# DeltaNet branch: the two directions' small products of both doublings issued alternately

## The chip, the cores and the metric

The kernel runs on one core of a Trainium2 chip. The metric is the time of one execution on the device in microseconds (us). The engines are TensorE (PE in the rows, its weight loads PEld), VectorE (DVE), ScalarE (ACT), GpSimd (POOL) and the DMA queues. Each engine takes its own instructions in the order in which the program has them, and semaphores tie the engines together.

## The reference, cut to what matters

One encoder layer: four token mixers, a gated merge, a memory cross attention and a mixture of experts, in float32. The change lies in the fourth mixer, a gated DeltaNet that runs over the sequence forward and backward. For each chunk of 64 tokens and each of 4 heads it solves a unit lower triangular system and then carries a state on:

```
a_mat = jnp.where(strict, bc[..., None] * kk * decay, 0.0) + jnp.eye(c)
sol = lax.linalg.triangular_solve(a_mat, rhs, left_side=True, lower=True, unit_diagonal=True)
...
o_f = gdn_scan(q, k, v, beta[:, :, 0], log_a[:, :, 0])
o_b = _flip(gdn_scan(_flip(q), _flip(k), _flip(v), ...))
```

## The kernel before

The kernel handles DeltaNet in 8 steps i of 128 tokens (two chunks of 64), for both directions d (0 forward, 1 backward) and NH = 4 heads h. VectorE has inverted the 32x32 diagonal blocks of each triangular matrix. Two doublings make the whole inverse of them: the first ("level 5") joins 32x32 blocks to 64x64, the second ("level 6") joins 64x64 blocks to 128x128. A doubling is a product y (L1023), a negated copy of it, and a product with it, zy (L1040); level 5 also has a third product xy (L1033), which makes the transposed block.

TensorE's part of a step is `gdn_c` with parts 0 to 6, all under `for d in range(2)`:

- part 0: `gbc` (L1014, two full-size products), then y of level 5. Per direction: wait for the copies of the step before, `gbc`, wait for GpSimd's `z` (L2807), y.
- part 1: wait for VectorE's `yn` (L2406, two instructions per direction), then xy and zy of level 5.
- part 2: wait for VectorE's `z` (L2411 once and L2413 twice per direction, which copy xy and zy out of PSUM), then y of level 6.
- part 3: wait for ScalarE's `yn` (L1731), then zy of level 6.
- part 4: wait for ScalarE's `z` (L1735), then `wk` (L1047), which ScalarE copies out (L1739).
- part 5: v (L1053, L1061); VectorE makes `vn` from it (L2419). Part 6: u and o (L1067, L1072, L1075); VectorE updates the state (L2424, L2429), and o is copied out by ScalarE (L1743) for i below 4, by VectorE (L2432) from i = 4 on. The next step's `gbc` of the same direction waits for that copy.

The small products of level 5 are 32x32 on 32 rows and 32 columns of the array, those of level 6 64x64. The operands' partitions fix the place:

```
OFF = ((slice(64, P), slice(0, 64)), (slice(0, 64), slice(64, P)))
OFF32 = [[(slice(64 * b + 32, 64 * b + 64), slice(64 * b, 64 * b + 32))[::1 - 2 * d] for b in range(2)] for d in range(2)]
```

So a level-5 y or zy uses two 32x32 places of the array for one direction and two others for the other direction; xy uses one place for each direction; a level-6 product uses one 64x64 place for each direction. A float32 product is two passes (two MATMUL rows of the trace). The semaphore of TensorE's DeltaNet work is one counter that rises in program order.

The order of all engines' work is a hand-written list of steps. Between the parts it puts pieces of the merge projection (L787, six 128x512 products, "a filler"): one filler after each of parts 1 to 5, none between parts 0 and 1 and none between part 6 and the next part 0. In steps 0 to 2 VectorE also has pieces of the second half's block inversion (L2385, L2388) after parts 1, 2 and 4. After part 2 (from step 1 on) ScalarE issues the loads of the next step (L1774, L1782).

Of the kernel before, what the change touches and what calls it, by code (L numbers as in the profile page):

```python
# [29 lines left out]
NH = 4  # L30
# [273 lines left out]
def build(nc, A, out, known):  # L304
# [15 lines left out]
    with ExitStack() as ctx:  # L320
# [435 lines left out]
        def _(pe):  # L756
            for step in schedule:
# [240 lines left out]
                elif what == "gdn_c":  # L998
# [3 lines left out]
                    for d in range(2):  # L1002
# [13 lines left out]
                        if part in (0, 2):  # L1016
                            if part == 0:
                                pe.wait_ge(*po.at("z", i, d))
                            else:
                                pe.wait_ge(*v.at("z", i, d, 5))  # L1020
                            for h in range(NH):
                                for rows_y, cols_y in OFF32[d] if part == 0 else (OFF[d],):
                                    mm = nc.tensor.matmul(B0[rows_y, h, cols_y], NLT[s][d][cols_y, h, rows_y], NX[d][cols_y, h, cols_y],  # L1023
                                                          start=True, stop=True)
                            mm.then_inc(*q.mark("y", i, d, 5 + part // 2))
                        elif part in (1, 3):
                            lv = 5 + part // 2
                            pe.wait_ge(*(v if lv == 5 else a).at("yn", i, d, lv))
                            if lv == 5:
                                pe.wait_ge(*a.at("qd", i, d))  # L1030
                                rows_y, cols_y = OFF32[d][d]
                                for h in range(NH):
                                    mm = nc.tensor.matmul(B1[rows_y, h, cols_y], NZ_[d][rows_y, h, rows_y], NY[d][rows_y, h, cols_y],  # L1033
                                                          start=True, stop=True)
                                mm.then_inc(*q.mark("xy", i, d, lv))
                                if i:
                                    pe.wait_ge(*v.at("um", i - 1, d))
                            for h in range(NH):
                                for rows_y, cols_y in OFF32[d] if lv == 5 else (OFF[d],):
                                    mm = nc.tensor.matmul(B2[cols_y, h, rows_y], NY[d][rows_y, h, cols_y], NZ_[d][rows_y, h, rows_y],  # L1040
                                                          start=True, stop=True)
                            mm.then_inc(*q.mark("zy", i, d, lv))
# [1901 lines left out]
```

## Time and profile before

| what | value |
|---|---|
| time, 3 runs | 2054.76 us median (2052.96 to 2055.24) |
| the profiled execution's own time | 2065.67 us |
| its span, first to last instruction | 2063.9 us |
| TensorE busy | 1909.5 us, 93% of the span |
| VectorE / ScalarE / GpSimd busy | 1388.5 / 1083.7 / 324.1 us |
| L1023 on TensorE (y, both levels) | 384 passes in 15.0 us |
| L1040 on TensorE (zy, both levels) | 384 passes in 14.7 us |

The eight steps of parts 0 to 6 lie between 792 and 957 us of the span. A row of the timeline gives the start of a group of instructions, the time from the first start to the last end, and in brackets how long the engine had been idle before it and what released it. Since passes of TensorE overlap, a group's time less the last pass's own time is the time between its first and last start.

### The profile page before, as it was taken

The numbers are of one execution on the slowest core, as the hardware profiler recorded it, in microseconds if no ns is written. First come the engines' busy times: TensorE is split into PE (matmuls) and PEld (weight loads), VectorE is DVE, ScalarE is ACT, GpSimd is POOL, SyncE is SP. The second block draws the span as 40 slices with busy tenths as digits, with TensorE's granted clock in tenths as the row PEclk, the third lists the DMA queues.
The fourth block names the chain that finished last, engine by engine and source line by source line (L and its number), as shares of the span: only waits on it lengthen the run. The fifth ranks groups of instructions, "written<-read, shape, count | busy, mean of one in ns | idle before, by whom it ended". The sixth has DMA issues, their size and how long they took to land.

```text
span 2063.9 us, 33015 instructions
## 1 busy us (share of the span) xinstructions
PE 1909.5 (93%) x13076; PEld 1138.2 (55%) x13076; DVE 1388.5 (67%) x1831; ACT 1083.7 (53%) x1582; POOL 324.1 (16%) x285
## 2 busy tenths in 40 slices
PE   6999999999999999999999999895899999999991
PEld 3464565655544545767488855685355444444440
DVE  4555533799865687634643845437799999999986
ACT  4563223666656432223333534334588888888862
POOL 6000100344300523421000000000001111111102
PEclk9999999999999999999999999997899999999995
DMA  5411111212011352332321500403799999999976
GB/s 185 161 51 42 32 42 53 66 47 57 24 39 47 118 179 83 113 108 99 138 67 48 168 32 21 167 31 152 268 423 422 422 422 421 422 422 422 422 290 261
DMA packets 140522, 360.45 MB, mean 175 GB/s; under 512 B 38224, under 2 KB 91632, under 8 KB 113776
## 3 DMA queue, kind: packets, MB, share of 16 engines
q1 hardware_dynamic: 96608, 279.57, 35.7%
q10 hardware_dynamic: 34944, 46.14, 6.4%
q0 software_dynamic: 8848, 33.03, 4.1%
q8 instruction: 87, 1.43, 0.3%
q14 instruction: 35, 0.29, 0.0%
HBM read 307.85 MB, written 46.66 MB: 172 GB/s over the span
## 4 chain that ended last, share of the span: by engine, by line
PE 79%; DVE 9%; ACT 5%; issue 4%; DMA 1%; SPq 1%; DVEq 0%; ACTq 0%; POOL 0%; POOLq 0%
PE psum L787 40%; PE psum L1194 24%; ACT arena L1636 2%; PE psum L1183 1%; PE psum L1118 1%; PE psum L1093 1%; DVE arena L2288 1%; PE psum L917 1%; PE psum L1212 1%; PE psum L804 1%; PE psum L1053 1%; PE psum L989 1%; DMA arena<-in_w_in_dram 1%; PE psum L979 1%; PE psum L928 1%
## 5 line engine op out<-in xcount | busy, mean ns | idle before, releaser
L787 PE MATMUL psum<-arena 128*128 128x512 f16 (+2 forms) x6000 | 1016.6, 327 | 7.7 <-issue 2.8
L787 PEld LDWEIGHTS psum<-arena 128*128 128x128 f16 x6000 | 569.6, 98 | 391.5 <-issue 23.5
L1194 PE MATMUL psum<-arena 128*128 128x512 f16 x2304 | 513.5, 382 | 15.6 <-issue 12.5
L744 DVE SCALAR_TENSOR_TENSOR arena<-arena 128x2048 f16<-128x2048 f32 x192 | 437.6, 2286 | 57.9 <-ACT arena L738 57.6
L738 ACT ACTIVATE arena<-arena 128x2048 f16<-128x2048 f32 x192 | 365.5, 1908 | 69.6 <-DMA arena<-in_w_dram 42.9
L1194 PEld LDWEIGHTS psum<-arena 128*128 128x128 f16 x2304 | 224.7, 98 | 282.4 <-issue 24.7
L1944 DVE SCALAR_TENSOR_TENSOR arena<-arena 128x512 f16<-128x512 f32 (+1 forms) x185 | 124.9, 695 | 123.0 <-ACT arena L1358 122.6
L2847 POOL DMA_INDIRECT arena<-xhat,arena x32 | 67.5, 2109 | 842.1 <-PE psum L1183 446.0
L1358 ACT ACTIVATE arena<-arena 128x512 f16<-128x512 f32 (+1 forms) x212 | 127.0, 616 | 35.8 <-PE psum L787 11.4
L1379 ACT ACTIVATE arena<-psum,arena 128x512 f32<-128x512 f32 x64 | 43.8, 684 | 149.2 <-PE psum L787 149.1
L1443 ACT ACTIVATE arena<-psum 128x512 f32<-128x512 f32 (+3 forms) x51 | 29.9, 586 | 119.8 <-PE psum L787 119.8
L1407 ACT ACTIVATE arena<-arena 128x256 f32<-128x256 f32 x64 | 26.6, 416 | 108.9 <-DVE arena L1980 107.9
L2735 POOL TENSOR_SCALAR arena<-arena 128x512 f32<-128x512 f32 x27 | 57.5, 2129 | 138.8 <-ACT arena L1358 138.8
L2273 DVE CUSTOM_DVE_ANT_0 arena<-psum,arena 128x1024 f32<-128x1024 f32 x64 | 75.6, 1219 | 2.1 <-PE psum L904 2.0
L1968 DVE SCALAR_TENSOR_TENSOR arena<-arena,psum 128x512 f32<-128x512 f32 x64 | 43.8, 684 | 49.0 <-PE psum L787 34.8
L1636 ACT ACTIVATE arena<-arena 128x1024 f32<-128x1024 f32 x64 | 72.9, 1147 | 7.1 <-DVE arena L2273 7.0
L1998 DVE SCALAR_TENSOR_TENSOR arena<-psum,arena 128x512 f16<-128x512 f32 x36 | 24.8, 690 | 61.5 <-ACT arena L1443 31.0
L1980 DVE SCALAR_TENSOR_TENSOR arena<-psum,arena 128x512 f32<-128x512 f32 x32 | 22.1, 690 | 64.3 <-PE psum L787 64.3
L1645 ACT ACTIVATE arena<-psum 128x512 f16<-128x512 f32 x64 | 34.7, 595 | 55.1 <-PE psum L917 34.3
L2807 POOL TENSOR_TENSOR arena<-arena 128x512 f32<-128x512 f32 x32 | 34.8, 1106 | 128.0 <-DMA arena<-gdn_inv 82.6
L1859 ACT ACTIVATE arena<-psum 128x512 f32<-128x512 f32 x64 | 38.1, 597 | 14.2 <-PE psum L1194 13.9
L1183 PE MATMUL psum<-arena 128*128 128x128 f32 x256 | 34.4, 278 | 10.3 <-DMA arena<-xhat,arena 10.3
(390 smaller groups left out, 2089.6 us busy)
## 6 DMA issues: line engine op xcount, KB each, us to landing
arena<-in_w_dram SPq DMA_DIRECT2D x192, 1024.0 KB, 11.9
arena<-in_merge_w_dram SPq DMA_DIRECT2D x64, 256.0 KB, 3.0
yrows<-arena ACTq DMA_DIRECT2D x32, 512.0 KB, 7.9
arena<-in_w_in_dram SPq DMA_DIRECT2D x48, 256.0 KB, 2.8
gdn_lq<-arena ACTq DMA_DIRECT2D x8, 1024.0 KB, 4.0
arena<-gdn_lq ACTq DMA_DIRECT2D x8, 1024.0 KB, 5.1
arena<-in_xattn_wkv_dram SPq DMA_DIRECT2D x32, 256.0 KB, 2.8
yrows<-arena POOLq DMA_DIRECT2D x1, 7680.0 KB, 24.3
```

The lines of the kernel that those rows point to most:

```text
L738: nc.scalar.activation(half_of(pieces(e, m)[0], half), half_of(XLAND[m], half), ACT.Copy, scale=WS).then_inc(w_hi[m], 1)
L744: nc.vector.scalar_tensor_tensor(half_of(lo, half), half_of(XLAND[m], half), WS, half_of(hi, half), ALU.mult, ALU.subtract).then_inc(w_lo[ ...
L787: mm = nc.tensor.matmul(bank[prt[0]:prt[1], c0:c1], lhs[a](k), rhs[b](k), start=(k == 0 and a + b == 0), stop=(k == nk - 1 and a == 1))
L1183: tr = nc.tensor.transpose(PS[:, k // 4, (k % 4) * P:(k % 4) * P + P], xs[:, k, :], ident)
L1194: mm = nc.tensor.matmul(PS[:, bank, :], left[a][:, k, :], right[b][:, k, columns], start=k + a + b == 0, stop=(k == n - 1 and a == 1))
L1358: S.activation(W[i % 2][0][:, 2 * j:2 * j + 2, 0:wide], LAND[c % NLAND][:, :, 0:wide], ACT.Copy, scale=WS).then_inc(*act_hi.mark(c))
L1379: S.activation(SG[gate_no[n] % 2], bank, ACT.Tanh, scale=0.5 / WS, bias=half_b[:, 8 * kind[1] + kind[2]:8 * kind[1] + kind[2] + 1]).then_i ...
L1636: S.activation(DS[u % 2][:, m, :], DS[u % 2][:, m, :], ACT.Exp, scale=-1.0, bias=d_mx[u % 2][:, m:m + 1], accum_out=d_l[u % 2][:, m:m + 1])\
L1944: V.scalar_tensor_tensor(W[i % 2][1][:, 2 * j:2 * j + 2, 0:wide], LAND[c % NLAND][:, :, 0:wide], WS, W[i % 2][0][:, 2 * j:2 * j + 2, 0:wid ...
L2273: V.tensor_tensor_reduce(out=DS[u % 2][:, m, :], in0=PS[:, 2 + 2 * m:4 + 2 * m, :].rearrange("p a b -> p (a b)"), in1=DWH[:, 896 - P * qt: ...
L2735: G.tensor_scalar(landed_c, landed_c, WS, None, ALU.mult).then_inc(*counter("pool_w_scaled").mark(chunk))
L2847: G.indirect_dma_start(XR[e % 2], None, XH_D, bass.IndirectOffsetOnAxis(IDX[:, e:e + 1], 0)).then_inc(rows_in[e % 2], 16)
```

## The change

The per-direction loop keeps the waits and the full-size products. The small products of both levels are taken out of it and issued after it, head by head and direction by direction within a head. So all waits of both directions now stand ahead of the first small product of a part. No instruction is added or taken away, and the lists of VectorE, ScalarE, GpSimd and the DMA queues are as they were.

```diff
                         if part in (0, 2):
-                            if part == 0:
-                                pe.wait_ge(*po.at("z", i, d))
-                            else:
-                                pe.wait_ge(*v.at("z", i, d, 5))
-                            for h in range(NH):
-                                for rows_y, cols_y in OFF32[d] if part == 0 else (OFF[d],):
-                                    mm = nc.tensor.matmul(B0[rows_y, h, cols_y], NLT[s][d][cols_y, h, rows_y], NX[d][cols_y, h, cols_y],
-                                                          start=True, stop=True)
-                            mm.then_inc(*q.mark("y", i, d, 5 + part // 2))
+                            pe.wait_ge(*(v.at("z", i, d, 5) if part else po.at("z", i, d)))
                         elif part in (1, 3):
-                            lv = 5 + part // 2
-                            pe.wait_ge(*(v if lv == 5 else a).at("yn", i, d, lv))
-                            if lv == 5:
+                            pe.wait_ge(*(a.at("yn", i, d, 6) if part == 3 else v.at("yn", i, d, 5)))
+                            if part == 1:
                                 pe.wait_ge(*a.at("qd", i, d))
...
+                    if part in (0, 2):
+                        for h in range(NH):
+                            for d in range(2):
+                                for rows_y, cols_y in of[d]:
+                                    mm = nc.tensor.matmul(bank[d][0][rows_y, h, cols_y], NLT[s][d][cols_y, h, rows_y], NX[d][cols_y, h, cols_y],
+                                                          start=True, stop=True)
+                                if h == NH - 1:
+                                    mm.then_inc(*q.mark("y", i, d, 5 + part // 2))
+                    if part == 1:
+                        for h in range(NH):
+                            for d in range(2):
+                                rows_y, cols_y = OFF32[d][d]
+                                mm = nc.tensor.matmul(bank[d][1][rows_y, h, cols_y], NZ_[d][rows_y, h, rows_y], NY[d][rows_y, h, cols_y],
+                                                      start=True, stop=True)
+                                if h == NH - 1:
+                                    mm.then_inc(*q.mark("xy", i, d, 5))
+                    if part in (1, 3):
+                        for h in range(NH):
+                            for d in range(2):
+                                for rows_y, cols_y in of[d]:
+                                    mm = nc.tensor.matmul(bank[d][2][cols_y, h, rows_y], NY[d][rows_y, h, cols_y], NZ_[d][rows_y, h, rows_y],
+                                                          start=True, stop=True)
+                                if h == NH - 1:
+                                    mm.then_inc(*q.mark("zy", i, d, 5 + part // 2))
```

On TensorE, parts 0 and 1 of one step stand like this before (a row is a run of like instructions; the names in brackets are the semaphores waited for: `pool_gdn`, `vec_gdn`, `act_gdn` are the DeltaNet counters of GpSimd, VectorE and ScalarE):

```order
L1014 MATMUL psum<-arena 128x128 [waits pool_gdn,act_gdn,vec_gdn]
L1014 MATMUL psum<-arena 128x128
L1023 MATMUL psum<-arena 32x32 [waits pool_gdn]
L1023 MATMUL psum<-arena 32x32 x7
L1014 MATMUL psum<-arena 128x128 [waits pool_gdn,act_gdn,vec_gdn]
L1014 MATMUL psum<-arena 128x128
L1023 MATMUL psum<-arena 32x32 [waits pool_gdn]
L1023 MATMUL psum<-arena 32x32 x7
L1033 MATMUL psum<-arena 32x32 [waits act_gdn,vec_gdn]
L1033 MATMUL psum<-arena 32x32 x3
L1040 MATMUL psum<-arena 32x32 [waits vec_gdn]
L1040 MATMUL psum<-arena 32x32 x7
```

And in the changed kernel, whose L1066, L1074 and L1082 are y, xy and zy:

```order
L1014 MATMUL psum<-arena 128x128 [waits pool_gdn,act_gdn,vec_gdn]
L1014 MATMUL psum<-arena 128x128
L1014 MATMUL psum<-arena 128x128 [waits act_gdn,pool_gdn,vec_gdn]
L1014 MATMUL psum<-arena 128x128
L1066 MATMUL psum<-arena 32x32 [waits pool_gdn]
L1066 MATMUL psum<-arena 32x32 x15
L1074 MATMUL psum<-arena 32x32 [waits vec_gdn,act_gdn]
L1074 MATMUL psum<-arena 32x32 x7
L1082 MATMUL psum<-arena 32x32 x16
```

The forward direction's y now stands behind the backward direction's `gbc` and its waits, and its xy and zy behind the backward direction's `yn`.

Parts 2 and 3 on TensorE, before:

```order
L1023 MATMUL psum<-arena 64x64 [waits vec_gdn]
L1023 MATMUL psum<-arena 64x64 x3
L1023 MATMUL psum<-arena 64x64 [waits vec_gdn]
L1023 MATMUL psum<-arena 64x64 x3
L787 MATMUL psum<-arena 128x512 x6
L1040 MATMUL psum<-arena 64x64 [waits act_gdn]
L1040 MATMUL psum<-arena 64x64 x3
L1040 MATMUL psum<-arena 64x64 [waits act_gdn]
L1040 MATMUL psum<-arena 64x64 x3
```

And now, at the same place of a step:

```order
L1066 MATMUL psum<-arena 64x64 [waits vec_gdn]
L1066 MATMUL psum<-arena 64x64 x7
L787 MATMUL psum<-arena 128x512 [waits vec_w_lo]
L787 MATMUL psum<-arena 128x512 x5
L1082 MATMUL psum<-arena 64x64 [waits act_gdn]
L1082 MATMUL psum<-arena 64x64 x7
```

What was one direction's four products and then the other's is now eight in alternation behind the waits of both (the filler's own wait, for the merge's weights, is one that it has in either kernel).

## Rows read from the trace of the kernel before

**Rows 1.** The page: the span, and the chain that ended last, by engine.

```profile
span 2063.9 us, 33015 instructions
...
PE 79%; DVE 9%; ACT 5%; issue 4%; DMA 1%; SPq 1%; DVEq 0%; ACTq 0%; POOL 0%; POOLq 0%
```

**Rows 2.** TensorE's waits, 790 to 950 us: us in total, times, longest us.

```profile
PE psum L1033 <- DVE arena L2406: 4.4, 8, 1.5
PE psum L1047 <- ACT arena L1735: 2.3, 2, 1.4
PE psum L1014 <- DVE arena L2432: 1.9, 4, 0.6
PE psum L1014 <- POOL arena L2820: 1.1, 1, 1.1
```

**Rows 3.** Timeline of TensorE, step 1, parts 0 and 1.

```profile
813.11 0.44 PE L1023 MATMUL psum<-arena 32*32 32x32 f32 x16
...
816.06 0.34 PE L1033 MATMUL psum<-arena 32*32 32x32 f32 x5 [1.50 <-DVE arena L2406]
...
816.69 0.34 PE L1033 MATMUL psum<-arena 32*32 32x32 f32 x5
...
817.22 1.47 PE L787 MATMUL psum<-arena 128*128 128x512 f16 x6
```

**Rows 4.** TensorE, step 1, part 2, cut at 818.895, at 819.08, and whole.

```profile
818.62 0.44 PE L1023 MATMUL psum<-arena 64*64 64x64 f32 x4
...
818.62 0.67 PE L1023 MATMUL psum<-arena 64*64 64x64 f32 x11
...
818.62 0.96 PE L1023 MATMUL psum<-arena 64*64 64x64 f32 x16
```

**Rows 5.** Timeline of VectorE, step 1: `yn`, then the copies of part 1.

```profile
815.39 1.24 DVE L2406 TENSOR_SCALAR arena<-psum 32x128 f32<-32x128 f32 x4
816.70 0.28 DVE L2411 COPY arena<-psum 32x128 f32<-32x128 f32 x1
...
817.85 0.61 DVE L2413 COPY arena<-psum 32x128 f32<-32x128 f32 x2
```

**Rows 6.** Timeline of TensorE, step 6, parts 0 and 1.

```profile
915.93 0.68 PE L1014 MATMUL psum<-arena 128*128 128x128 f32 x4 [0.34 <-DVE arena L2432]
916.54 0.34 PE L1023 MATMUL psum<-arena 32*32 32x32 f32 x10
...
917.69 0.34 PE L1033 MATMUL psum<-arena 32*32 32x32 f32 x5 [0.39 <-DVE arena L2406]
...
918.21 1.47 PE L787 MATMUL psum<-arena 128*128 128x512 f16 x6
```

**Rows 7.** Timeline of VectorE, step 6: o, then `yn` of both directions.

```profile
915.42 0.41 DVE L2432 TENSOR_TENSOR arena<-psum,arena 128x256 f32<-128x256 f32 x1
915.86 0.61 DVE L2406 TENSOR_SCALAR arena<-psum 32x128 f32<-32x128 f32 x2
917.03 0.60 DVE L2406 TENSOR_SCALAR arena<-psum 32x128 f32<-32x128 f32 x2 [0.56 <-PE psum L1023]
```

**Rows 8.** Timeline of ScalarE, step 6, parts 2 and 3.

```profile
922.01 0.69 ACT L1379 ACTIVATE arena<-psum,arena 128x512 f32<-128x512 f32 x1 [0.91 <-PE psum L787]
...
924.74 0.78 ACT L1735 ACTIVATE arena<-psum 64x256 f32<-64x256 f32 x2 [2.04 <-issue]
```

**Rows 9.** VectorE busy, 804 to 828.9 us: us, busy and count, clock, DMA.

```profile
804.00:828.90 24.90, 23.43 (x56) 1.00 0.23 65
```

**Rows 10.** Timeline, end of step 1: `vn` on VectorE and the weight load that waits.

```profile
828.92 0.76 DVE L2419 TENSOR_TENSOR arena<-psum,arena 128x256 f32<-128x256 f32 x2
829.40 0.53 PEld L1067 LDWEIGHTS psum<-arena 128*128 128x128 f32 x4 [0.22 <-DVE arena L2419]
```

**Rows 11.** Timeline of ScalarE, step 4, part 2: the loads of the next step.

```profile
879.64 2.79 ACTq L1782 DMA_DIRECT2D arena<-gdn_inv  x2
```

**Rows 12.** Timeline of TensorE, step 5: a filler and the part 2 behind it.

```profile
897.18 2.74 PE L787 MATMUL psum<-arena 128*128 128x512 f16 x6
899.85 1.26 PE L1023 MATMUL psum<-arena 64*64 64x64 f32 x16
```

**Rows 13.** TensorE in that stretch: us, busy and count, granted clock, DMA.

```profile
897.00:901.00 4.00, 4.00 (x41) 0.57 0.00 0
```

More of the change, by code:

```diff
@@ L1016, in _ @@
                         if part in (0, 2):
-                            if part == 0:
-                                pe.wait_ge(*po.at("z", i, d))
-                            else:
-                                pe.wait_ge(*v.at("z", i, d, 5))
-                            for h in range(NH):
-                                for rows_y, cols_y in OFF32[d] if part == 0 else (OFF[d],):
-                                    mm = nc.tensor.matmul(B0[rows_y, h, cols_y], NLT[s][d][cols_y, h, rows_y], NX[d][cols_y, h, cols_y],
-                                                          start=True, stop=True)
-                            mm.then_inc(*q.mark("y", i, d, 5 + part // 2))
+                            pe.wait_ge(*(v.at("z", i, d, 5) if part else po.at("z", i, d)))
                         elif part in (1, 3):
-                            lv = 5 + part // 2
-                            pe.wait_ge(*(v if lv == 5 else a).at("yn", i, d, lv))
-                            if lv == 5:
+                            pe.wait_ge(*(a.at("yn", i, d, 6) if part == 3 else v.at("yn", i, d, 5)))
+                            if part == 1:
                                 pe.wait_ge(*a.at("qd", i, d))
[L1031 to L1035, printed above, removed]
                                 if i:
                                     pe.wait_ge(*v.at("um", i - 1, d))
[L1038 to L1042, printed above, removed]
                         elif part == 4:
@@ L1078, in _ @@
                             mm.then_inc(*q.mark("o", i, d))
+                    bank = [[PS[:, 2 + 3 * d + b, :].rearrange("p (h n) -> p h n", h=NH) for b in range(3)] for d in range(2)]
+                    of = [OFF32[d] if part < 2 else (OFF[d],) for d in range(2)]
+                    if part in (0, 2):
[22 more added lines that the diff above has]
+                                    mm.then_inc(*q.mark("zy", i, d, 5 + part // 2))
                 elif what == "xattn_s":
```

## The prediction

> **What bounds the kernel now.** I read the page first: TensorE makes 79% of the chain that ended last [rows 1]. The change touches only the eight DeltaNet steps between 792 and 957 us, so the second view is who TensorE waits for there [rows 2]: for VectorE's `yn` (L2406) once in every step, 4.4 us, for ScalarE's `z` (L1735) twice, 2.3 us, and ahead of `gbc` (L1014) for the last copy of the step before, 1.9 and 1.1 us. Everything else in the stretch is TensorE's own work back to back. So a saving on TensorE counts if no other engine's result is late behind it, and a result that VectorE gives later counts as soon as no filler covers it. Then come the timelines of a step, TensorE beside VectorE, once for the early steps [rows 3, 5] and once for the late ones [rows 6, 7].
>
> **What alternation gives.** A group's time less its last pass is the time from first to last start. Level 6, 16 passes: the first 4 start within 0.44 - 0.22 = 0.22 us, the next 7 within 0.23 us (0.67 - 0.44), the last 5 within 0.29 us [rows 4]. The outer stretches have one direction running, about 58 ns a pass; in the middle both run and together start one in 33 ns at most (7 in 0.23). So the two 64x64 places work side by side without slowing each other, and today they overlap for only about three passes. In full alternation 8 passes of each need 8 x 58 = 0.46 us in place of 0.96 - 0.22 = 0.74 us: 0.28 us less. There are 16 such groups (parts 2 and 3 of 8 steps): 4.5 us off TensorE. Level 5 with one direction already uses two places: 16 passes in 0.44 - 0.19 = 0.25 us [rows 3], one start in 17 ns, against 0.15/4 = 37 ns where xy has one place alone (L1033 x5 in 0.34 us). No row has four places at work; I take it that they scale on, 32 passes in 0.25 us. Then part 1 for both directions takes what it takes for one now: from the start at 816.69 to the filler at 817.22, 0.53 us [rows 3].
>
> The Trainium skill, page "TensorE: Matmul & The Clock Gate", section "Wait — 56ns, not 53.3ns?", says that start to start never drops below about 25 ns however small the product. Its rule would leave level 5 nothing to gain; this trace disagrees at two places already, 17 ns, and it leaves level 6 alone, whose alternate starts are 29 ns apart.
>
> **What alternation costs, part by part.**
>
> Parts 0 and 1. In steps 1 to 3 VectorE is busy with the state until 815.39 while both y were done by 814.56, so the later forward y costs nothing, and `yn` of both directions still ends at 815.39 + 1.24 = 816.63 [rows 3, 5]. In the late steps it is otherwise. In step 6 VectorE makes the forward `yn` at 915.86, while TensorE is still at the backward `gbc`, which waited for L2432 [rows 6, 7]. Now the forward y stands behind that `gbc`: both y start at 916.54, end 0.25 + 0.19 us later, and VectorE starts the first `yn` where it now starts the second, at 917.03. One direction's `yn` (0.31 us x 2 = 0.62) moves from under the wait to behind it. Part 1 starts at 917.69 + 0.62. The same holds for steps 5 and 7, and for step 0 with GpSimd's L2820 in the place of L2432 [rows 2]. In step 4 the copy is ScalarE's and comes earlier: from the same chain I get 0.27. Sum on part 1's start: 4 x 0.62 + 0.27 = 2.75 us.
>
> Part 2. It waits for six copies on VectorE, three a direction. In step 1 they run from 816.70 to 817.85 + 0.61 = 818.46 [rows 5], because the forward products are done before the backward ones start. TensorE arrives at 818.62, hence 0.16 us of slack [rows 4]. Now no copy can begin before the joint part 1 is through: start 816.69, last start 0.40 later, 0.19 for the pass, 0.05 for the semaphore (816.63 to 816.69 above): 817.33. The six end at 817.33 + 1.76 = 819.09, part 2 starts at 819.14 in place of 818.62: 0.53 us in each step that is not stopped otherwise. What covers it now is the filler of 1.40 us, and that is too short by this much.
>
> **The steps added up** (change of TensorE's time, each step on top of the one before):
>
> - Step 0: 0.62 + 0.53 - 0.56 = +0.6.
> - Step 1: 0.53 - 0.56 = 0.0 at first. But VectorE is 1.2 us later and has almost no idle time to lose it, 23.43 us busy of 24.90 [rows 9]; `vn` ends at 829.68 and L1067's weights have already waited for it [rows 10]. So +0.5.
> - Step 2: ScalarE's `z` is already late by 1.4 us [rows 2]. ScalarE's chain hangs on the filler behind part 2 (L1379 in [rows 8] for step 6, alike here), which moves by 0.53 - 0.28; the saving of part 3 falls into that wait. +0.25.
> - Step 3: 0.53 - 0.56 = 0.0.
> - Step 4: 0.27 + 0.53 - 0.56 = +0.25 if ScalarE keeps up. Its load issues take 2.79 us behind L1731 [rows 11] and then release L1735; if they keep their length, the later part 2 comes through whole, +0.8. I take the middle, +0.5.
> - Step 5: the filler ran at half clock and took 2.74 us [rows 12], so it covers the copies: 0.62 - 0.56 = +0.05.
> - Step 6: 0.62 + 0.53 - 0.28 = +0.9, as in step 2, since L1379 and then L1735 stand on the filler [rows 8].
> - Step 7: 0.62 + 0.53 - 0.56 = +0.6.
>
> Sum +3.4 us. Behind the stretch TensorE leads the chain, so I let it through to the end whole. Bounds from the same rows: if VectorE's `vn` in step 1 and ScalarE in step 4 do not bite, +2.6; if step 5 has no slow filler, that step costs 0.53 more, and with step 4 at its upper end +4.2. Removing the two switches between small and full-size products in part 0 lies wholly under VectorE's work, hence nothing.
>
> **The clock.** In step 5 the granted clock fell to 0.5 of full (1.2 of 2.4 GHz; 0.57 is the mean of the stretch [rows 13]) right behind parts 0 and 1 of that step, in which TensorE has little but small products and waits, as in [rows 6]. It cost (2.74 - 1.47) + (1.26 - 0.96) = 1.6 us [rows 12]. The change makes just these thin stretches 0.6 us longer in four steps, so one more such drop is likely in some runs. I add 0.4 us for it, a quarter of a drop: +3.8 us. The profiled execution (2065.67 us) would become 2069.5; on the median, 2054.8 + 3.8 = 2058.6 us.
>
> **The rivals.**
>
> - Waits already there take it all. If joint y comes out before VectorE is free in the late steps too, and part 2's copies are not last, the 4.5 us of level 6 stay whole: 2050.3 us, faster. It decides at 0.16 us of slack ahead of part 2 [rows 4, 5]: the copies may begin no more than that later. Against it: VectorE's idle 0.56 us ahead of the backward `yn` [rows 7] shows that it does wait for y. 7%.
> - The gains and losses cancel, 2054 to 2056 us. If joint part 1 ends earlier than I take it (all its passes at 8 ns, 48 x 8 = 0.38 us at most), or the forward copies may start some 0.3 us sooner, part 2 loses 0.2 in place of 0.53. 13%.
> - Four places do not scale. If TensorE starts one level-5 pass in 17 ns at best, joint y takes 0.53 in place of 0.25 and joint part 1 0.80 in place of 0.40 us; that is 5 x 0.28 + 8 x 0.40 = 4.6 us more: 2063.2 us. No row excludes it. 8%. By the skill's 25 ns it would be 32 x 25 = 0.80 and 48 x 25 = 1.20 us, thus 5 x 0.55 + 8 x 0.80 = 9.2 us more, 2067.8 us; since a row has 17 ns I give it 1%.
> - One or two more clock drops in the median run: 1.6 us each, 2060.2 to 2061.8 us. 16%.
> - The forecast, 2057.2 to 2059.8 us: 55%.
>
> About 0.2% (4.1 us) is what a measurement of this kernel can tell from no change, and the forecast lies just inside it. Slower by more than that: the clock, the four places, and somewhat under half of the forecast's own range: 0.48. Within it: the rest of the forecast and the cancelling case, 0.45. Faster: 0.07. The range from 2054.5 to 2062.5 leaves out the first rival, the four places and some of the clock.
>
> **What would show it.** Level-6 groups at 0.68 us in place of 0.96 (right about the array); L1074 starting at least 0.6 us later behind `gbc` in steps 0, 5, 6 and 7 and not in 1 to 3; a new TensorE wait ahead of the 64x64 products for L2413's successor, 0.4 to 0.6 us in most steps, 3 to 4 us in sum; joint y of 32 passes at 0.44 us. It would be wrong if that wait is not there, or if the level-5 groups of 32 passes take 0.7 us and more.

## The result, and the profile after

The changed kernel takes 2069.72 us (median, 2067.86 to 2071.63) where the kernel before, on the same chip, takes 2053.86 us (2052.58 to 2055.24). The medians differ by 15.9 us, the kernel is **slower**; the ratio is 1.0073 (15.0 us), 95% interval 1.0057 to 1.0090. In a second measurement it was 1.0078 (1.0062 to 1.0093), and the medians differed by 15.8 us. The prediction said 2058.6 us, 2054.5 to 2062.5: the sign was right, the size a quarter of the real one, and the time is outside the range.

The page of the changed kernel, its span and the chain that ended last; these answer to [rows 1]:

```profile
span 2068.5 us, 33046 instructions
...
PE 78%; DVE 10%; ACT 5%; issue 4%; DMA 1%; SPq 1%; POOL 0%; DVEq 0%; ACTq 0%; POOLq 0%
```

The page hardly moved; the stretch of the DeltaNet steps did. Its ends are in the timeline of TensorE. Before, the first level-5 products and the last `o` products:

```profile
792.88 0.44 PE L1023 MATMUL psum<-arena 32*32 32x32 f32 x16
...
953.86 1.00 PE L1075 MATMUL psum<-arena 128*128 128x64 f32 x8
```

After, the same two:

```profile
792.12 0.45 PE L1066 MATMUL psum<-arena 32*32 32x32 f32 x32
...
966.11 1.00 PE L1056 MATMUL psum<-arena 128*128 128x64 f32 x8
```

From the first product to the start of the last one the stretch took 161.7 us before and 174.7 after, **13.0 us more**. The two profiled spans differ by less (4.6 us) because before's profiled execution lay 11 us above its median: behind the stretch, where both kernels do the same work, it took 1109.3 us, the changed kernel 1101.6. From here on "the stretch" is this piece, and every kernel is compared by it and by its ratio.

TensorE's waits in the stretch, 790 to 955 us, for [rows 2] (us in total, times, longest us):

```profile
PE psum L1074 <- DVE arena L2413: 14.0, 8, 2.6
PE psum L1014 <- DVE arena L2439: 3.8, 4, 1.2
PE psum L1028 <- ACT arena L1742: 3.0, 2, 1.8
PE psum L1066 <- DVE arena L2420: 1.6, 3, 0.5
PE psum L1014 <- POOL arena L2827: 1.3, 1, 1.3
PE psum L1048 <- DVE arena L2426: 0.8, 1, 0.8
```

L1074 is part 1 (before L1033), L2413 is `yn` (L2406), L1066 is y (L1023), L2439 the copy that `gbc` waits for (L2432). The wait of part 1 grew from 4.4 to 14.0 us, yet that is not a loss of 9.6: before, the forward products were done while TensorE waited for the backward `yn`, and now all eight steps wait with nothing in hand.

The granted clock, 792 to 952 us, first before, then after (us, busy time and count of PE, PEld, DVE, ACT and POOL, granted clock, DMA share, GB/s):

```profile
792.00:952.00 160.00, 150.09 (x1755) 110.62 (x1754) 89.82 (x238) 39.01 (x91) 56.59 (x77) 0.99 0.28 85
```

```profile
792.00:952.00 160.00, 135.89 (x1640) 96.01 (x1640) 86.70 (x233) 35.06 (x82) 53.57 (x73) 0.93 0.28 82
```

TensorE was busy 14 us less of the same 160 us, and its mean clock fell from 0.99 to 0.93. In the clock records of the trace the stretch of before has 3.4 us at the half level (1.2 of 2.4 GHz), that of after 23.9 us, in six places; four of them begin within 1.3 us of the start of part 1 of a step (steps 1, 3, 6 and 7), one begins 1.1 us ahead of it (step 5, 6.8 us long), and one lies in the middle of step 2. Over the whole execution the difference is small in these two profiles, 118.8 us at the half level before and 122.3 after; what a typical execution of before has is a matter of the control run below.

How one step looks now: TensorE in step 4, parts 0, 1, the filler and part 2, to be held against [rows 3, 4]:

```profile
879.82 0.37 PE L1066 MATMUL psum<-arena 32*32 32x32 f32 x24
881.84 0.34 PE L1074 MATMUL psum<-arena 32*32 32x32 f32 x11 [1.65 <-DVE arena L2413]
...
882.48 1.47 PE L787 MATMUL psum<-arena 128*128 128x512 f16 x6
884.49 0.68 PE L1066 MATMUL psum<-arena 64*64 64x64 f32 x16 [0.54 <-DVE arena L2420]
```

And VectorE beside it, `yn` of both directions and the six copies, for [rows 5]:

```profile
880.23 1.24 DVE L2413 TENSOR_SCALAR arena<-psum 32x128 f32<-32x128 f32 x4 [1.06 <-PE psum L1066]
882.58 0.28 DVE L2418 COPY arena<-psum 32x128 f32<-32x128 f32 x1 [1.11 <-PE psum L1082]
...
883.73 0.61 DVE L2420 COPY arena<-psum 32x128 f32<-32x128 f32 x2
```

Three things stand in these seven rows. The level-6 group takes 0.68 us in place of 0.96. TensorE begins part 1 at 881.84, but `yn` had ended at 880.23 + 1.24 = 881.47: 0.37 us, where before the same gap was 0.06 (816.63 to 816.69). The trace has this in other steps too: 0.05 to 0.06 us in all eight before, 0.36 to 0.39 in steps 1 to 7 and 0.26 in step 0 after. And part 2 waits 0.54 us for the copies although a filler stands ahead of it (1.40 us from its start to the next work).

TensorE in step 6, for [rows 6]:

```profile
922.63 0.68 PE L1014 MATMUL psum<-arena 128*128 128x128 f32 x4 [0.81 <-DVE arena L2439]
923.25 0.45 PE L1066 MATMUL psum<-arena 32*32 32x32 f32 x32
925.35 0.37 PE L1074 MATMUL psum<-arena 32*32 32x32 f32 x11 [1.65 <-DVE arena L2413]
...
926.12 2.74 PE L787 MATMUL psum<-arena 128*128 128x512 f16 x6
928.79 0.74 PE L1066 MATMUL psum<-arena 64*64 64x64 f32 x16
```

From the backward `gbc` to part 1 it is 2.72 us now, 1.76 before. The filler of six products takes 2.74 us, as in [rows 12] and not 1.47: the half clock. Because it lasts longer, part 2 behind it shows no wait.

### The profile page after: what moved, and what is told of

It reads as the page before. It is cut to its first block, busy times and chain, and to the rows that moved or that the text cites. A ratio compares the mean times of both kernels' runs of the same rounds, so it can differ in the third digit from the quotient of the medians.

```text
span 2068.5 us, 33046 instructions
## 1 busy us (share of the span) xinstructions
PE 1907.4 (92%) x13076; PEld 1133.0 (55%) x13076; DVE 1387.6 (67%) x1831; ACT 1084.1 (52%) x1582; POOL 322.8 (16%) x285
## 4 chain that ended last, share of the span: by engine, by line
PE 78%; DVE 10%; ACT 5%; issue 4%; DMA 1%; SPq 1%; POOL 0%; DVEq 0%; ACTq 0%; POOLq 0%
PE psum L787 40%; PE psum L1201 24%; ACT arena L1643 2%; PE psum L1190 1%; PE psum L1100 1%; PE psum L1125 1%; DVE arena L2295 1%; PE psum L917 1%; PE psum L804 1%; PE psum L1219 1%; PE psum L989 1%; PE psum L979 1%; DVE arena L2395 1%; DMA arena<-in_w_in_dram 1%; PE psum L928 1%
## 5 line engine op out<-in xcount | busy, mean ns | idle before, releaser
L787 PE MATMUL psum<-arena 128*128 128x512 f16 (+2 forms) x6000 | 1021.5, 328 | 7.1 <-DVE arena L2090 2.8
L787 PEld LDWEIGHTS psum<-arena 128*128 128x128 f16 x6000 | 570.0, 99 | 393.2 <-issue 28.2
L1866 ACT ACTIVATE arena<-psum 128x512 f32<-128x512 f32 x64 | 38.1, 597 | 14.2 <-PE psum L1201 14.1
## 6 DMA issues: line engine op xcount, KB each, us to landing
arena<-in_w_dram SPq DMA_DIRECT2D x192, 1024.0 KB, 11.9
```

What stands on the lines that cost most here:

```text
L787: mm = nc.tensor.matmul(bank[prt[0]:prt[1], c0:c1], lhs[a](k), rhs[b](k), start=(k == 0 and a + b == 0), stop=(k == nk - 1 and a == 1))
```

## The experiments

All ratios are to the kernel before on the same chip, with a 95% interval. That kernel's own median was 2061.1, 2059.8 and 2061.4 us on chips A, B and C and 2053.9 to 2054.7 us on chip D ("first" is the chip of the result above), so times are not compared across chips. "Stretch" and "half clock" (the time at the lower level within the stretch) come from one profiled execution each; they are compared across chips, so differences of a few us between them are to be read with care. My theory: the waits (the joint starts, and several semaphore waits in a row at them) and the clock share the loss. The rivals: one part alone carries it, the alternation itself costs, or the clock is chance.

| kernel | chip | ratio | interval | stretch us | half clock us |
|---|---|---|---|---|---|
| after, and again | first, D | 1.0073, 1.0078 | 1.0057-1.0090, 1.0062-1.0093 | 174.7, 173.1 | 23.9, 23.9 |
| before, and again | first, C | 1 | | 161.7, 166.2 | 3.4, 13.7 |
| level 6 only | A | 0.9991 | 0.9969-1.0013 | 159.8 | 10.2 |
| level 5 only, twice | A, D | 1.0080, 1.0081 | 1.0054-1.0105, 1.0061-1.0101 | 174.8, 175.9 | 20.5, 27.3 |
| part 0 only, twice | C, D | 1.0010, 1.0024 | 0.9996-1.0025, 1.0007-1.0040 | 170.9, 166.9 | 17.1, 10.2 |
| part 1 only, twice | C, D | 1.0016, 1.0026 | 1.0003-1.0029, 1.0011-1.0042 | 175.7, 170.8 | 23.9, 17.1 |
| joint, not alternated | A | 1.0090 | 1.0065-1.0115 | 181.1 | 27.3 |
| after, few waits | A | 1.0050 | 1.0029-1.0071 | 173.3 | 23.9 |
| after, five extra products | B | 1.0039 | 1.0021-1.0056 | 167.3 | 0.0 |
| after, filler behind part 0 | B | 1.0021 | 1.0009-1.0033 | 166.7 | 20.5 |
| before, filler behind part 0 | B | 0.9999 | 0.9985-1.0014 | 164.8 | 20.5 |
| level 6 only, filler there | B | 1.0021 | 1.0007-1.0036 | 161.8 | 13.7 |
| level 6, few waits | D | 0.9985 | 0.9972-0.9999 | 158.4 | 6.8 |
| level 6, few waits, extra products | C | 0.9974 | 0.9956-0.9992 | 159.5 | 3.4 |
| before, extra products | D | 0.9978 | 0.9967-0.9989 | 160.5 | 0.0 |

**Which level.** The condition of the joint waits and of the alternation is narrowed; the other parts keep their form of before.

```diff
-                    if part in (0, 2):
+                    if part in (0, 2) and part in (2, 3):
...
-                    if part in (1, 3):
+                    if part in (1, 3) and part in (2, 3):
```

> Only level 6 (parts 2 and 3) is alternated, parts 0 and 1 are as before. Theory A (the loss is all in the joint level 5: the forward half of yn and of the copies comes later, and the clock drops in the longer idle stretches): the array's gain of 0.28 us in each of 16 groups is kept, less what falls into ScalarE's two waits, and VectorE's z of both directions is ready 0.16 us before TensorE comes, so 2050 to 2051.5 us, faster than before by 2.5 to 4 us, with about one clock drop between 790 and 960 us. Theory B (alternation on the array is itself bad, or the gathered waits of level 6 cost as much as it gives): 2054 us or more.

With (0, 1) in place of (2, 3):

> Only level 5 (parts 0 and 1) is alternated. Theory A: the whole loss of the changed kernel and 3 to 4 us more, since level 6 gives nothing back: 2072 to 2074 us, with five or more clock drops between 790 and 960 us. Theory B: part of the loss only, 2062 to 2066 us.

Level 5 alone costs as much as the whole change, 0.80%; level 6 alone is a small gain or nothing. The loss sits in parts 0 and 1.

**Joint starts or alternation.** The joint waits stay, the loop over directions goes outside the loop over heads, in all three groups alike:

```diff
-                        for h in range(NH):
-                            for d in range(2):
+                        for d in range(2):
+                            for h in range(NH):
```

> The waits stand gathered as in the changed kernel, but within a group the small products come direction by direction. Theory A (waits and clock cost, alternation gives): as slow as the changed kernel or up to 4 us slower, 2069 to 2074 us; the 64x64 groups take 0.96 us again in place of 0.68. Theory B (alternation on the array is what costs): near the kernel before, 2054 to 2060 us.

The loss is all there without alternation, 0.90%, so it is not in the alternate order but in waiting for both directions before either begins. That alternation gives back part of it is seen in the groups (zy of level 6 takes 0.96 us again, and the stretch is 6 to 8 us longer, with 3.4 us more at half clock); the ratio alone, whose interval overlaps that of the changed kernel, does not show it.

**The waits in a row.** Part 1 had six semaphore waits ahead of its first product (`yn`, ScalarE's `qd` and `um`, a product of VectorE's state update in the step before; one of each per direction); here it waits once per counter, for the later value. Parts 0, 2 and 3 wait once in place of twice for their small products as well:

```diff
-                        if part in (0, 2):
-                            pe.wait_ge(*(v.at("z", i, d, 5) if part else po.at("z", i, d)))
-                        elif part in (1, 3):
-                            pe.wait_ge(*(a.at("yn", i, d, 6) if part == 3 else v.at("yn", i, d, 5)))
-                            if part == 1:
-                                pe.wait_ge(*a.at("qd", i, d))
-                                if i:
-                                    pe.wait_ge(*v.at("um", i - 1, d))
+                        if part in (0, 2) and d:
+                            pe.wait_ge(*(v.at("z", i, 1, 5) if part else po.at("z", i, 1)))
+                        elif part == 1 and d:
+                            pe.wait_ge(*a.at("qd", i, 1))
+                            pe.wait_ge(*v.at("yn", i, 1, 5))
+                        elif part == 3 and d:
+                            pe.wait_ge(*a.at("yn", i, 1, 6))
```

> The changed kernel with one wait in place of several: since each engine's counter rises in order, waiting for the backward direction's value contains the forward one's, and ScalarE's qd is waited for before VectorE's yn. Theory A1 (each further wait that stands behind the blocking one costs 0.1 us on TensorE's queue: three in part 1, one in part 2): 0.3 + 0.1 us less in each of 8 steps, 3 us, and as the idle stretches are shorter perhaps one or two clock drops less: 2064 to 2067 us. Theory A2 (the gap of 0.36 us between yn and the first product has another cause): no change, 2069 to 2070 us.

Timeline of this kernel, `yn` on VectorE, then part 1 on TensorE:

```profile
819.02 1.24 DVE L2412 TENSOR_SCALAR arena<-psum 32x128 f32<-32x128 f32 x4
```

```profile
820.41 0.34 PE L1073 MATMUL psum<-arena 32*32 32x32 f32 x11 [2.52 <-DVE arena L2412]
```

819.02 + 1.24 = 820.26 to 820.41: 0.15 us in place of 0.37, and so in all eight steps. In the raw trace of the changed kernel three semaphore instructions stand on TensorE's queue between the end of `yn` (881.476) and the first product (881.839), at 881.515, 881.626 and 881.732: the first is the one that was held, the others had nothing left to wait for and still took 0.106 to 0.111 us each. With few waits one is left, at 820.300. The time confirms it less sharply: 1.0050 against 1.0073 and 1.0078, with overlapping intervals, and a stretch as long as before the edit. In its profile the wait for `vn` is 2.5 us where it was 0.8, about what the shorter hand-offs of part 1 give (1.6 us in sum). The time at half clock is the same 23.9 us, so hand-offs 0.2 us shorter did not move it.

**The clock.** Behind part 0, while TensorE would wait for `yn` anyway, it makes five full-size fp32 products whose result is overwritten unread:

```diff
+                    if part == 0:
+                        if i:
+                            pe.wait_ge(*v.at("um", i - 1, 0))
+                        for _n in range(5):
+                            nc.tensor.matmul(PS[:, 4, 0:P], st_f, inc_f, start=True, stop=True)
```

> The changed kernel, and between part 0 and the wait of part 1 five extra full-size float32 products (ten passes, about 1.1 us) of constants into a part of a PSUM bank that nothing reads; they are work that no result needs and lie inside an idle stretch of 1.2 us and more. Clock theory (about half of the 15 us is the clock, which falls because these stretches hold little but small products): the time at half clock between 790 and 970 us falls from 24 us to 7 us or less, and the kernel becomes 5 to 8 us faster than the changed one, a ratio to before of 1.003 to 1.005. Rival (the clock is incidental, the waits are all): no gain, ratio 1.007 or more.

The granted clock of this kernel over the same 160 us, and two of its waits:

```profile
792.00:952.00 160.00, 143.75 (x1788) 105.82 (x1789) 87.57 (x235) 38.03 (x89) 54.06 (x74) 1.00 0.28 84
```

```profile
PE psum L1066 <- DVE arena L2425: 4.3, 8, 0.5
PE psum L1074 <- DVE arena L2418: 3.8, 8, 1.3
```

Work that nobody needs went into the kernel and its ratio was 1.0039 where it had been 1.0073 and 1.0078 (another chip; the intervals 1.0021-1.0056 and 1.0057-1.0090 just do not meet): the half clock is gone from the stretch entirely. The products cost next to nothing, since they lie in the wait: summed over the eight steps part 1 starts 0.2 us later behind `gbc` than in the changed kernel. And with no slow filler left to cover it, part 2 now waits in all eight steps, 4.3 us, longest 0.5.

**Real work in the wait.** One filler (six products of L787) is planned behind part 0 as well, in three kernels:

```diff
-            gdn += [("gdn_c", i, part)] + [None] * (1 <= part < 6)
+            gdn += [("gdn_c", i, part)] + [None] * (part < 6)
```

> The changed kernel with the same filler between parts 0 and 1. Waits and clock theory: the filler covers about 1.3 of the 1.75 us of waiting ahead of part 1 in each step, 10 us, and takes away most of the clock drops, 6 to 8 us; the kernel then is about as fast as before or a few us faster, ratio 0.997 to 1.000. Rival (the alternation harms otherwise): ratio 1.004 or more.

> The kernel before with one filler of six merge products also between parts 0 and 1 (eight of the fillers that came after the stretch move forward; no work is added). If TensorE's 4.4 us of waiting for yn can be covered by moved work: 3.5 to 5 us faster than before, ratio 0.998, and no or one clock drop in the stretch. If VectorE is the real bound there (its copies start later, so part 2 waits instead): no change.

> Only level 6 alternated, and the filler between parts 0 and 1: the gains of both add up if they are independent, 6 to 8 us faster than before, ratio 0.996 to 0.997. If the later part 1 makes the copies late for part 2, part of it is lost: ratio 0.998.

The changed kernel then is at 1.0021, under a third of its loss and between what both sides had named; the kernel before gains nothing; and with level 6 alone, where 0.996 to 0.998 was expected, it is 1.0021, a plain miss: slower than before. The expectation had the moved work wrong: no filler comes forward from behind the stretch. The stretch has 240 products of L787 with the edit as without it, but 36 in each of steps 0 to 5, 24 in step 6 and none in step 7, where it was 30 in each. So step 7 stands without a filler, and there the clock falls: 13.7 us at the half level from 938.9 on in the kernel before with the filler, 17.1 of 20.5 us in the changed one, 6.8 of 13.7 with level 6 alone. The experiment thus moved the weak place as much as it filled one. The timeline of the kernel before with the filler has part 2 and part 3 of step 7 at 2.07 and 1.78 us for what was 0.96:

```profile
939.89 2.07 PE L1023 MATMUL psum<-arena 64*64 64x64 f32 x16
941.76 1.78 PE L1040 MATMUL psum<-arena 64*64 64x64 f32 x16
```

**Is the clock chance?** The kernel before once more:

> The kernel before once more, for a second profile of it. Theory A (the clock falls in few places of this stretch in the kernel before, and in many with the change): the stretch from the first 32x32 product of the sum to the last exit is again 160 to 164 us, with no more than 10 us of it at the half clock, and a profiled execution nearer to the median than 11 us. Theory B (the half-clock windows are chance and the profiles of before and after drew differently): 15 to 25 us at the half clock and a stretch of 168 to 175 us here too.

```profile
792.00:952.00 160.00, 149.91 (x1723) 108.78 (x1721) 88.96 (x235) 38.39 (x90) 55.31 (x76) 0.96 0.28 83
```

In part, yes: 13.7 us of half clock and a stretch of 166.2 us, between what both theories had named. My first reading of one profile, 3.4 against 23.9 us, had overstated the difference; the kernel before already loses clock here in some executions. These two executions also price it, roughly: 4.5 us more stretch for 10.3 us more at the half level, 0.44 us per us. The Trainium skill, page "TensorE: Matmul & The Clock Gate", section "Terms", puts the penalty at the slow time times one minus the granted share, which is one half of it at the lower of the two levels. This pair is near that; the kernels with waits lie lower (from 174 us and 23.9 to 167.3 and none, 0.28), and a wait is time in which TensorE has no work that the clock could stretch.

The mean granted clock is on record for every execution, and it says more than the profiles. On chip D the 23 executions of before have 0.9746 on average, the six of the changed kernel 0.9690: in time at the half level, 2 x (1 - clock) x span, 104.5 us and 128.2 us over the whole execution, **24 us more**. On chip A the three kernels with joint level-5 parts have 129 to 130 us, before 113. The two profiled executions of before, with 118.8 and 120.8 us, lie above the averages of before on all four chips (104 to 114 us), which goes with their being slower than its medians. Among the 23 executions of before themselves the time rises by 0.29 us per us at the half level (0.23 to 0.35 in the sets of the other chips), and the time of the program behind the stretch, the same work in all six kernels profiled on chip D, by 0.41 (from 1096.3 us with 72.6 to 1102.9 with 86.7). At 0.29 to 0.44 the 24 us are 7 to 10 us of the changed kernel's 15.8: an estimate from these numbers, but one that needs no single profile.

**The two halves of level 5,** each part alone, on two chips:

> Only the sum's level-5 part (part 0) is joint and alternated; the other parts stand direction by direction as before. Theory A (the waits of the prediction and the stacked waits are additive, and the clock follows the idle time): 2.75 us for the four steps with the late second copy and step 4, some 0.2 us of stacked waits in each of them, and one or two more half-clock windows: a ratio of 1.002 to 1.004. Theory B (part 0 alone carries the loss): a ratio of 1.006 to 1.009 and as many half-clock windows as the whole change has, 20 us or more at the half clock. Theory C (part 1 carries it): within 0.1% of before.

> Only the scaled level-5 products (part 1) are joint and alternated. Both directions wait for the second evacuation of the sum and for both copies. Theory A (additive): 0.53 us later for the first direction's copy and some 0.3 us of stacked waits in each of eight steps, 6.6 us, and one to three more half-clock windows: a ratio of 1.004 to 1.006. Theory B (part 0 carries the loss): within 0.1% of before. Theory C (part 1 carries all of it): a ratio of 1.006 to 1.009 with 20 us or more at the half clock.

> Part 0 alone joint and alternated, again. Theory A (the waits add: 2.2 us at part 1 and 1.4 us at the gate broadcast, and the clock follows in one to three more windows of 1.6 us): on a chip where the kernel before takes 2054 us, a ratio of 1.002 to 1.004. Theory B (the loss is more than its parts: one part alone leaves the array's work dense enough): 1.000 to 1.0015 on any chip.

> Part 1 alone joint and alternated, again. Theory A (5.4 us more of waits at part 1, and three to five more windows at the half clock of 1.6 us each): on a chip where the kernel before takes 2054 us, a ratio of 1.004 to 1.006. Theory B (the loss is more than its parts): 1.0005 to 1.002 on any chip.

Each part alone costs something (of part 0 only the second measurement excludes zero), neither costs all. The additive theory had 1.004 to 1.006 for part 1, which is missed both times (1.0016 and 1.0026), and 1.002 to 1.004 for part 0, which the first time misses (1.0010) and the second meets (1.0024). On the second chip 0.24% and 0.26% make 0.50%, where both together have 0.81% on the same chip. Waits nearly add: the wait ahead of part 1 is 4.4 us before, 6.6 with part 0, 9.5 to 9.8 with part 1, 14.0 to 14.2 with both (11.9 if they only added). That the loss is more than the sum of its parts is likely but not shown; from the intervals the sum of the two may reach some 0.7%, and both together may cost as little as 0.61%.

**The whole and level 5 once more,** and two versions that might beat both kernels. In the version of level 6 without and with extra products, each of parts 2 and 3 has one wait; the products (three, two and two behind part 0 of steps 1 to 3, two ahead of `gbc` of steps 5 to 7) were then put into the kernel before as well.

```diff
+                            if i >= 5 and d:
+                                for _n in range(2):
+                                    nc.tensor.matmul(PS[:, 4, 0:P], st_f, inc_f, start=True, stop=True)
...
+                    if part == 0 and i in (1, 2, 3):
+                        pe.wait_ge(*v.at("um", i - 1, 0))
+                        for _n in range(3 if i == 1 else 2):
+                            nc.tensor.matmul(PS[:, 4, 0:P], st_f, inc_f, start=True, stop=True)
```

> The whole change once more, in more runs and on the same chip as the three beside it. Theory A (the loss is a joint effect of both level-5 waits, and the clock follows): a ratio of 1.005 to 1.008. Theory B (the parts add: part 0 cost 0.1%, part 1 0.16%, level 6 gained 0.1%, and the first measurement drew a chip or a clock that was dear): 1.001 to 1.003.

> Only parts 0 and 1 are joint and alternated, once more. Theory A (the two waits act together: each joint start delays the other direction's copies, which the next joint part waits for): a ratio of 1.006 to 1.009, over twice the sum of the two parts alone. Theory B (additive): 1.002 to 1.004.

> Only level 6 alternates, each of its parts waits once for the last of its sources instead of once per source, and fp32 products of full size that compute nothing wanted stand in the idle places: three after part 0 of step 1, two after that of steps 2 and 3, two ahead of the gate broadcast of steps 5 to 7. Theory A (level 6's alternation saves 0.28 us twice a step, 4.5 us, and the rest is clock): a ratio of 0.996 to 0.998, 4 to 8 us faster than before, with no more than 3 us at the half clock and a stretch of 153 to 157 us. Theory B (the alternation of level 6 gains nothing, because the copies behind it are what is late): a ratio of 0.999 to 1.001 with a stretch of 159 to 162 us, whatever the clock does.

> Only level 6 alternates, each of its parts waits once, for the last of its sources, and there are no extra products. Theory A (level 6's alternation gains 4.5 us, less what the clock takes): a ratio of 0.997 to 0.999. Theory B (the gain in the version with extra products was the clock's): 0.999 to 1.001, with 7 to 14 us at the half clock in the stretch.

> The kernel before with the same full-size products in the idle places as the version with level 6 alone had (three after part 0 of step 1, two after that of steps 2 and 3, two ahead of the gate broadcast of steps 5 to 7), and no alternation. Theory A (the gain of that version is level 6's alternation): a ratio of 0.999 to 1.001. Theory B (the gain is the clock's alone, since even the kernel before loses 3 to 14 us of this stretch to the half clock): a ratio of 0.996 to 0.998, with no more than 3 us at the half clock and a stretch of 158 to 161 us.

The granted clock of the kernel before with these products, and its wait ahead of part 1:

```profile
792.00:952.00 160.00, 153.86 (x1793) 115.47 (x1793) 90.39 (x243) 38.76 (x90) 53.98 (x74) 1.00 0.29 85
```

```profile
PE psum L1036 <- DVE arena L2413: 2.6, 6, 0.6
```

The products alone make the kernel before 0.22% faster (4.4 us), and with level 6 alternated it is 0.26% on another chip. Both beat both kernels; which of the two is the better is not told apart, and level 6 without extra products gains 0.15% (its interval, 0.01 to 0.28%, just leaves out zero). Theory B of the last expectation, for the kernel before with extra products, held: no half clock in the stretch and a gain from the products alone. Over the whole execution its time at the half level falls from 104 to 90 us. The gain that I had claimed for level 6 in the version with both is therefore mostly the clock's: its ratio came out as expected, its stretch (159.5 where 153 to 157 was said) did not. Without the extra products the stretch of level 6 was still the shortest of all, 158.4 us with 6.8 at the half clock.

## Why the prediction was wrong

Two terms of the sum failed, and both were too small: the clock (0.4 us, measured 7 to 10) and the waits of the level-5 parts (+3.4 us for the whole sum without the clock, measured about 7). Point by point, as it put them:

- **What alternation gives**: right. Level-6 groups take 0.68 us as said. The four 32x32 places work side by side: 32 passes in 0.45 us [rows 3: 16 in 0.44], 31 starts in 0.26 us or 8 ns each. The rival "four places do not scale" is out. The Trainium skill, page "TensorE: Matmul & The Clock Gate", section "Wait — 56ns, not 53.3ns?", whose 25 ns from start to start were weighed there, is contradicted more strongly than before.
- **Part 1 later in the late steps**: the mechanism is right, the size short. Behind the backward `gbc` the backward direction's part 1 starts 0.96 us later in step 6 (2.72 against 1.76), where 0.62 was said. The rest is the hand-off: I took 0.05 us from a place with one wait, and the six of part 1 leave three instructions behind each other here. That is 0.31 us in each of seven steps and 0.20 in step 0, 2.4 us that no term held. Step 4 behaves like the late ones (0.93 where 0.27 was said), and steps 1 to 3, which were to lose nothing, have 0.4 to 0.6. Over the eight steps part 1 starts 6.2 us later behind `gbc`, where the sum had 2.75. Ahead of the backward `gbc` it is alike: in step 5 the copy on VectorE ends at 899.82 and L1014 starts at 900.08, 0.26 where it was 0.10:

```profile
899.41 0.41 DVE L2439 TENSOR_TENSOR arena<-psum,arena 128x256 f32<-128x256 f32 x1
```

```profile
900.08 0.68 PE L1014 MATMUL psum<-arena 128*128 128x128 f32 x4 [1.08 <-DVE arena L2439]
```

- **Part 2 later by 0.53 us in every step**: right in kind, somewhat short. From the filler's start to part 2 it is 2.01 us (882.48 to 884.49) where 1.93 was worked out, and part 1 itself takes 0.64 us to the filler (881.84 to 882.48) where 0.53 was said. From the start of part 1 to part 2 at full clock it is 2.65 us in place of 1.93, 0.72 us more and not 0.53. Over eight steps that is 5.8 us for 4.2. The new wait was to be 3 to 4 us in sum and is 1.6, because slow fillers cover it in five steps; with the clock held it is 4.3.
- **Steps 1, 2 and 6**: right in kind. VectorE's `vn` bites (L1048, 0.8 us), and ScalarE's `z` wait takes up the saving of part 3 (3.0 us for 2.3).
- **The clock**: I gave 0.4 us, a quarter of one drop. The stretch has 23.9 us at the half level in both profiled executions of the changed kernel, against 3.4 and 13.7, and the whole execution has 24 us more on average. At 0.29 to 0.44 us per us that is 7 to 10 us. I had priced a drop rightly (1.6 us) and named the place, but reckoned with one rare drop: the profile of before showed one in eight steps, so I took the other seven as safe. They were not, neither in the changed kernel (six places) nor in the second profile of before (three).

The sum without the clock can be checked directly, since two kernels have no half clock in the stretch at all: the changed one with five extra products and the one before with its extra products. The first level-5 products and the last `o` products of each (the last product itself starts 0.7 us behind the start of its group):

```profile
792.67 0.45 PE L1066 MATMUL psum<-arena 32*32 32x32 f32 x32
...
959.21 1.00 PE L1056 MATMUL psum<-arena 128*128 128x64 f32 x8
```

```profile
790.30 0.44 PE L1026 MATMUL psum<-arena 32*32 32x32 f32 x16
...
950.04 1.00 PE L1078 MATMUL psum<-arena 128*128 128x64 f32 x8
```

That is 167.3 and 160.5 us, 6.8 us more, twice the +3.4 of the sum, and the extra products of the changed kernel account for about 0.2 of it. The measured shifts give much the same: 6.2 and 5.8 us later, less the 4.5 us that alternation gives, is 7.5. The ratio 1.0039 of the first of the two agrees (8 us, with an interval from 4 to 12). So the waits are about 7 us and the clock 7 to 10, together 14 to 17 where the medians say 15.8.

What stays open: the division is an estimate, from single profiles on different chips for the waits and from a price per us for the clock. Why the clock falls is known only as far as the experiments go: it falls in and behind thin places, full-size products put there keep it up, and waits shortened by 0.2 us change nothing. And whether parts 0 and 1 amplify each other was not settled.

## What to carry to other kernels

Merging two independent chains on the engine that sets the end makes each start wait for the later of both, and moves the first chain's work from under a wait to behind it: count that before the gain of the denser order. Put the extra semaphore waits into the sum too, and wait once for the later value. If the profile shows even one drop of TensorE's clock in a repeated pattern, price the change also with a drop in most repetitions, and compare the mean granted clock of many executions before trusting one profile. Unneeded full-size products in a wait that exists anyway are a cheap test of the clock, and here a small gain by themselves.

## What was unexpected in the hardware

- A semaphore instruction whose condition was already met took 0.106 to 0.111 us on TensorE's queue behind a held one; the two of them and the held one ahead made part 1 start 0.36 us after its data, 0.31 later than the one wait of before. With one instruction left it was 0.15 us in all eight steps.
- Four 32x32 places of the array take passes at 8 ns each (32 in 0.26 us from first to last start), two at 17 ns, one at 32 ns once it runs (the 37 ns of the prediction are the mean of four gaps, of which the first is 52).
- The granted clock fell in and behind groups of small tiled products and waits, and hardly at all in the three kernels that had full-size fp32 products there (0 of 167.3, 0 of 160.5 and 3.4 of 159.5 us), although nobody reads what these products compute.
- The same kernel had 3.4 and 13.7 us of half clock in the same stretch in two executions, and over whole executions of it the time at the half level goes with the time: 0.29 us per us in 23 executions. One profile does not tell how a kernel stands with the clock.
